# Hybrid attention block: scores of two pairs in one visit from pair 4 on, and the up tiles by token turned by DMA, with one transpose of the identity behind them

## The chip, the cores and the metric

The kernel runs on one core of one Trainium2 chip. The metric is the device time of one execution in microseconds (us), lower is better. Engines are named as in the profile: PE is TensorE (PEld its weight loads), DVE is VectorE, ACT is ScalarE, POOL is GpSimd, SP is SyncE, which here only issues transfers.

## The reference

Two layers (DEPTH = 2) over 256 tokens of 1024 values. Each layer projects x to three kinds of attention with 8 heads each, gates and merges their outputs, adds and normalises, and then runs a convolutional gated feed-forward block, adds and normalises again. Cut to what matters here:

```python
o_mla = _dense_causal_attention(q, k, kv[..., MLA_NOPE:], (MLA_NOPE + MLA_ROPE) ** -0.5, None)   # heads of 96
o_fox = _dense_causal_attention(f_q, f_k, f_v, HEAD_DIM ** -0.5, cumsum(log_f))                  # heads of 64
o_dsa = _dsa_attention(s_q, s_k, s_v, i_q, i_k, i_w, positions, slopes, topk)                    # heads of 64
# feed-forward: D_FF = 2816, CONV_WIDTH = 3
u = x @ w_up
gate, val = u[..., :D_FF], u[..., D_FF:]
conv = conv_b + sum(gp[:, j:j + seq] * conv_w[j] for j in range(3))   # gp: gate, padded by two tokens in front
y = (gelu(conv) * val) @ w_down
```

## The kernel before, in words

Every engine's program is written out by hand in one order, and engines meet through counting semaphores (`wait_ge`, `then_inc`). All large products are made in three matmuls, high by high, high by low and low by high part (`product`, L738 to L740), with the parts split by ACT (`split_hi`, L1248) and DVE (`split_lo`, L1607) for each weight panel of 128 x 2048 values. SP loads panels into a ring of 6 raw buffers; a slot is free when PE has used the panel six before.

**Attention.** The 24 heads form 12 pairs: pairs 0 to 3 are the fox heads (64 rows), 4 to 7 the MLA heads (96 rows), 8 to 11 the DSA heads (64 rows). PE runs through slots 0 to 27. In slots 0 to 23 it makes one gate tile (24 products), and behind it, where due, small plain fp32 work: `scores` of pair i in slot 2i + 1 (four matmuls in L1042, two passes each: for each of two token tiles one for each head of the pair), the probabilities' transposes for pairs 0 and 1 (L1057), and `values` of two pairs (L1080). Such a place, where PE leaves the products and comes back, is called a visit. Scores of every pair go to PSUM banks 0 and 1, so `scores(i)` waits until DVE has read pair i - 1. From pair 2 on the probabilities are turned by DMA: POOL splits the 32-bit words into two planes of 16 bits (`split_probs`, L2119), SP issues a transposing DMA (L698), and DVE or POOL joins the planes again. From slot 24 the branch panels follow.

**Feed-forward, up.** An up panel f gives 128 gate columns and 128 value columns. The first three panels are made by token (`up_by_token`: tokens in the rows of the result), because token tile 0 is normalised before tile 1. ACT copies their results to `u_tok` (L1372). PE then turns them into columns by 12 transposes (`turn_up`, L1146): 8 behind the last product by token, 4 behind panel 3. Panels 3 to 21 are made by column (`ffn_up`, 48 products each, moving x). For each panel ACT takes the first tap (`conv_first`, L1380), DVE the other two (`conv_rest`, L1868 and L1871), ACT the gelu (L1387), DVE multiplies (`hidden`, L1879), and both split the result (L1391, L1883). The same loops of ACT and DVE also split the weight panel two ahead, so a late step there delays weights.

## Time and profile before

| what | us |
|---|---|
| median of 3 runs (lowest to highest) | 825.98 (825.44 to 826.12) |
| the profiled execution | 826.03 |
| its span in the profile | 824.3 |
| PE busy | 812.5 (99%) |
| DVE busy | 596.5 (72%) |
| ACT busy | 469.6 (57%) |
| POOL busy | 177.3 (22%) |

The profile is of one execution. Its span is the time between the first and the last instruction; 1.73 us of the execution's 826.03 lie outside it. PE is busy nearly the whole span, and in the profile's chain of work that ended last it has 95%. A PE matmul row's duration is modelled and overlaps the next one's; what a product costs is the distance between the starts of two rows, called its pitch below.

### The profile page before, as it was taken

To read this page: it belongs to the slowest core of one execution; us is meant where nothing else is said; L and a number is where in the kernel's file an instruction comes from. 1 tells how busy PE (TensorE), PEld (TensorE's weight loads), DVE (VectorE), ACT (ScalarE), POOL (GpSimd) and SP (SyncE) were. 2 spreads that over 40 slices of the span, in tenths; PEclk is the share of its full clock that TensorE was granted. 3 is DMA by queue.
4 is the path that set the end of the run, shared out by engine and by line. 5 is a ranking of instruction groups with operands and counts; after the bars stand their busy time and mean duration, and the time that the engine had idled before them with its cause. 6 is when DMAs were issued, how large, how long until landed. Compare 5 with 4: busy or idle time off the path is not lost.

```text
span 824.3 us, 15624 instructions
## 1 busy us (share of the span) xinstructions
PE 812.5 (99%) x6215; PEld 759.0 (92%) x6215; DVE 596.5 (72%) x1012; ACT 469.6 (57%) x729; POOL 177.3 (22%) x193
## 2 busy tenths in 40 slices
PE   8999999999999999999999999999999999999996
PEld 7899999899899999988889999999998999999885
DVE  5675789878886777765676568998887587777555
ACT  5675876763446555543447578767544475555440
POOL 1502944439200000000000057333660000000000
PEclk9999999999999999999999999999999999999998
DMA  9959657767578776475846694778767776664731
GB/s 305 241 141 258 209 143 204 199 161 247 171 187 215 203 202 189 151 236 181 264 122 172 117 339 148 180 186 205 212 196 209 181 200 186 187 184 155 254 116 51
DMA packets 222266, 158.86 MB, mean 193 GB/s; under 512 B 64652, under 2 KB 196336, under 8 KB 221936
## 3 DMA queue, kind: packets, MB, share of 16 engines
q1 hardware_dynamic: 213120, 150.95, 65.2%
q10 hardware_dynamic: 9072, 6.90, 3.0%
q8 instruction: 49, 0.80, 0.4%
q14 instruction: 25, 0.20, 0.1%
HBM read 148.63 MB, written 1.06 MB: 182 GB/s over the span
## 4 chain that ended last, share of the span: by engine, by line
PE 95%; DVE 1%; SPq 1%; DMA 1%; ACT 1%; ACTq 1%; issue 0%; DVEq 0%
PE ps L738 29%; PE ps L740 29%; PE ps L739 29%; PE ps L1042 3%; PE ps L1080 2%; DMA raw<-w_in 1%; PE ps L817 1%; ACTq L1300 1%; DVE w_lo L1607 1%; ACT w_hi L1248 0%; PE ps L1004 0%; PE ps L1057 0%; PE ps L1146 0%; SPq L687 0%; DVE x_tok L1858 0%
## 5 line engine op out<-in xcount | busy, mean ns | idle before, releaser
L1607 DVE TENSOR_TENSOR w_lo<-raw,w_hi 128x2048 fp32r<-128x2048 f32 (+2 forms) x140 | 304.8, 2178 | 109.7 <-ACT w_hi L1248 109.5
L738 PE MATMUL ps<-xt_hi,w_hi 128*128 128x256 f32 x1232 | 346.0, 281 | 0.0
L739 PE MATMUL ps<-xt_lo,w_hi 128*128 128x256 f32 x1232 | 341.0, 277 | 0.0
L740 PE MATMUL ps<-xt_hi,w_lo 128*128 128x256 f32 x1232 | 341.0, 277 | 0.0
L1248 ACT ACTIVATE w_hi<-raw 128x2048 fp32r<-128x2048 f32 (+3 forms) x142 | 253.1, 1786 | 90.7 <-PE ps L740 67.9
L738 PEld LDWEIGHTS ps<-xt_hi,w_hi 128*128 128x128 f32 x1232 | 231.5, 188 | 5.8 <-issue 4.7
L739 PEld LDWEIGHTS ps<-xt_lo,w_hi 128*128 128x128 f32 x1232 | 231.5, 188 | 0.2
L740 PEld LDWEIGHTS ps<-xt_hi,w_lo 128*128 128x128 f32 x1232 | 231.5, 188 | 0.0
L738 PE MATMUL ps<-w_hi,ht_hi 128*128 128x512 f32 (+1 forms) x179 | 69.1, 386 | 0.0
L740 PE MATMUL ps<-w_hi,ht_lo 128*128 128x512 f32 (+1 forms) x179 | 69.0, 386 | 0.0
L739 PE MATMUL ps<-w_lo,ht_hi 128*128 128x512 f32 (+1 forms) x179 | 69.0, 386 | 0.0
L1380 ACT ACTIVATE cv<-ps,vec_t 128x256 f32<-128x256 f32 x44 | 20.8, 474 | 81.4 <-PE ps L740 77.8
L2148 POOL COPY km_t<-km_t 32x1792 f32<-32x1792 f32 x2 | 3.4, 1675 | 295.5 <-ACT km_t L1328 295.5
L1335 ACT ACTIVATE prob<-prob,least 128x128 f32<-128x128 f32 x96 | 42.5, 445 | 22.0 <-DVE least L1743 22.0
L738 PE MATMUL ps<-w_hi,xt_hi 128*128 128x256 f32 (+2 forms) x144 | 46.2, 321 | 0.6 <-DVE w_lo L1607 0.5
L740 PE MATMUL ps<-w_hi,xt_lo 128*128 128x256 f32 (+2 forms) x144 | 45.1, 313 | 0.0
L739 PE MATMUL ps<-w_lo,xt_hi 128*128 128x256 f32 (+2 forms) x144 | 45.0, 312 | 0.0
L1868 DVE SCALAR_TENSOR_TENSOR cv<-ps,vec_t,cv 128x255 f32<-128x255 f32 x44 | 21.3, 483 | 30.2 <-ACT cv L1380 29.9
L2179 POOL TENSOR_TENSOR merged<-merged,gated 128x256 f32<-128x256 f32 x32 | 40.2, 1287 | 5.3 <-DVE gated L1791 5.2
L740 PEld LDWEIGHTS ps<-w_hi,ht_lo 128*128 128x128 f32 x179 | 33.6, 188 | 6.7
L738 PEld LDWEIGHTS ps<-w_hi,ht_hi 128*128 128x128 f32 x179 | 33.6, 188 | 6.7
L739 PEld LDWEIGHTS ps<-w_lo,ht_hi 128*128 128x128 f32 x179 | 33.6, 188 | 6.7
(268 smaller groups left out, 1304.8 us busy)
## 6 DMA issues: line engine op xcount, KB each, us to landing
raw<-ffn_w_up SPq DMA_DIRECT2D x88, 512.0 KB, 5.2
raw<-w_in SPq DMA_DIRECT2D x84, 512.0 KB, 5.8
raw<-ffn_w_down SPq DMA_DIRECT2D x32, 512.0 KB, 4.2
raw<-w_branch SPq DMA_DIRECT2D x24, 512.0 KB, 4.6
raw<-w_out SPq DMA_DIRECT2D x16, 512.0 KB, 5.6
raw<-ffn_w_down SPq DMA_DIRECT2D x24, 256.0 KB, 3.0
decay<-decay_rows ACTq DMA_DIRECT2D x2, 1024.0 KB, 8.4
ln_g<-ln_g ACTq DMA_DIRECT2D x4, 512.0 KB, 3.6
```

Source lines behind the costliest of these rows:

```text
L738: pe.matmul(dst, a_hi, b_hi, start=first, stop=False)
L739: pe.matmul(dst, a_hi, b_lo, start=False, stop=False)
L740: return pe.matmul(dst, a_lo, b_hi, start=False, stop=last)
L817: ins = pe.transpose(ps[:, B_X[t][half], P * k:P * k + P], x_tok[:, t, P * kk:P * kk + P], ident[:])
L1042: ins = pe.matmul(ps[:, B_S[a], SPAN[t]], q[:, P * t:P * t + P], k[:, 0:P * (t + 1)], start=True, stop=True)
L1080: ins = pe.matmul(dst[HD * a:HD * a + HD, P * c:T], v, turned(i)[:, a, cols], start=c == 0, stop=c == 1)
L1248: ins = act.activation(panel_hi(l, p)[0:n, cols], panel_raw(l, p)[0:n, cols], ACT.Copy)
L1335: ins = act.activation(p, p, ACT.Exp, scale=-1.0, bias=least[:, i % 2, a, t:t + 1], accum_out=rsum[:, i % 2, a, t:t + 1])
L1380: act.activation(cv[:, buf, :], ps[:, B_UP[f % len(B_UP)], 0:T], ACT.Copy, scale=column(vec_t, V_CW + 2 * FT, f)).then_inc(s_conv_first_ta ...
L1607: ins = dve.tensor_tensor(low, panel_raw(l, p)[0:n, cols], panel_hi(l, p)[0:n, cols].bitcast(F32), ALU.subtract)
L1868: dve.scalar_tensor_tensor(cv[:, buf, 1:T], ps[:, B_UP[f % len(B_UP)], 0:T - 1], column(vec_t, V_CW + FT, f), cv[:, buf, 1:T], ALU.mult, A ...
L2179: pool.tensor_tensor(merged[:, u % KD, :], merged[:, u % KD, :], gated[:, u % NGATED, :], ALU.add).then_inc(s_merged_added, 1)
```

## The change

**Scores.** `PAIRED = range(4, 12)`: in the slot of an even pair i from 4 on, PE makes the scores of i and then of i + 1, in one visit. The odd pair writes to banks 2 and 3, which held the probabilities' transposes of pairs 0 and 1. DVE and ACT keep their slots.

**Up tiles.** `turn_up` is gone. POOL splits `u_tok` of each token tile into 16-bit planes (`split_up`), SP turns each tile by one transposing DMA (`cross_up`, behind the loads of panels 6 and 8), and POOL joins the planes into `u_feat` by 12 small copies (`join_up`). Behind the last product by token PE makes one transpose of the identity, whose result nobody reads, and goes on with panels 3 to 21. ACT and DVE take the tiles in the order 3, 4, 0, 5, 1, 6, 2, 7, ..., tiles 0 to 2 from SBUF.

```diff
+UP_ORDER = [3, 4, 0, 5, 1, 6, 2] + list(range(7, FT))
+UP_NO = [UP_ORDER.index(f) for f in range(FT)]
+PAIRED = range(4, PAIRS)
+B_S_ODD = (2, 3)
...
+        def score_bank(i, a):
+
+            return B_S_ODD[a] if i in PAIRED and i % 2 else B_S[a]
...
+            def cross_up(l, t):
+
+                sp.wait_ge(s_up_split, at("up_split", l, t + 1))
+                sp.dma_start_transpose(up_crossed[:, t], up_halves[:, t].rearrange("p u n -> p (u n)")).then_inc(s_up_crossed[t], 16)
...
+                    if p in (UP_AT + NLO, UP_AT + UP_BY_TOKEN - 1 + NLO):
+                        cross_up(l, p > UP_AT + NLO)
...
             def scores(l, i):
...
-                if i > 0:
+                if i > PAIRED.start + 1:
+                    pe.wait_ge(s_maxima_ready, at("maxima_ready", l, 2 * i - 2))
+                elif i == PAIRED.start + 1:
+                    pe.wait_ge(s_turned_even_ready, at("turned_even_ready", l, 2))
+                    pe.wait_ge(s_turned_odd_ready, at("turned_odd_ready", l, 2))
+                elif i > 0:
                     pe.wait_ge(s_maxima_ready, at("maxima_ready", l, 2 * i))
...
-                if f >= len(B_UP):
-                    pe.wait_ge(s_hidden_ready, at("hidden_ready", l, f - len(B_UP) + 1))
+                if f >= UP_BY_TOKEN + len(B_UP):
+                    pe.wait_ge(s_hidden_ready, at("hidden_ready", l, UP_NO[f - len(B_UP)] + 1))
+                elif f == UP_BY_TOKEN + len(B_UP) - 1:
+                    pe.wait_ge(s_up_tokens_ready, at("up_tokens_ready", l, NT * UP_BY_TOKEN))
...
                     for i in even_slot_pair(s, LAG_S):
-                        scores(l, i)
+                        if i not in PAIRED:
+                            scores(l, i)
+                        elif i % 2 == 0:
+                            scores(l, i)
+                            scores(l, i + 1)
...
-                turn_up(l, 0)
-                turn_up(l, 1)
-                ffn_up(l, 3)
-                turn_up(l, 2)
-                for f in range(4, FT):
+                pe.transpose(ps[:, B_R[0][1], 0:P], ident[:], ident[:])
+                for f in range(UP_BY_TOKEN, FT):
                     ffn_up(l, f)
...
-                for f in range(FT):
-                    if f >= 3:
+                for n, f in enumerate(UP_ORDER):
+                    if f >= UP_BY_TOKEN:
                         split_hi(*later(l, UP_AT + f, 2))
-                    if f >= 1:
-                        gelu(l, f - 1, (f - 1) % 2, f < 3)
-                    if f >= 2:
-                        hidden_hi(l, f - 2, f % 2)
-                    conv_first(l, f, f % 2)
+                    if n >= 1:
+                        gelu(l, n - 1, (n - 1) % 2, n < 3)
+                    if n >= 2:
+                        hidden_hi(l, n - 2, n % 2)
+                    conv_first(l, n, n % 2)
...
+            def split_up(l, t):
+
+                pool.wait_ge(s_up_tokens_ready, at("up_tokens_ready", l, UP_BY_TOKEN * (t + 1)))
+                pool.tensor_copy(up_halves[:, t], u_tok[:, t, :, :].rearrange("p f n -> p (f n)").bitcast(U16).rearrange(
+                    "p (n u) -> p u n", u=2)).then_inc(s_up_split, 1)
+
+            def join_up(l, f):
+
+                if f == 0:
+                    for t in range(NT):
+                        pool.wait_ge(s_up_crossed[t], 16 * (l + 1))
+                for t in range(NT):
+                    for i in range(2):
+                        src = up_crossed[:, t].rearrange("p (u b) k -> p u b k", u=2)[:, :, 2 * f + i, :]
+                        ins = pool.tensor_copy(u_feat[:, f, i, P * t:P * t + P].bitcast(U16).rearrange("p (k u) -> p u k", u=2), src)
+                ins.then_inc(s_up_joined, 1)
```

The order of PE's instructions in slots 17 to 19 of the first layer, before the change (sk_t and sq_t are the keys and queries of the DSA heads, L738 to L740 the products of the gate tiles):

```order
990 L1042 MATMUL ps<-sk_t,sq_t 128x128 x2
991 L1042 MATMUL ps<-sk_t,sq_t 128x256 x2
992 L738 MATMUL ps<-xt_hi,w_hi 128x256
...
1039 L740 MATMUL ps<-xt_hi,w_lo 128x256
1040 L1042 MATMUL ps<-sk_t,sq_t 128x128 x2
1041 L1042 MATMUL ps<-sk_t,sq_t 128x256 x2
1042 L738 MATMUL ps<-xt_hi,w_hi 128x256
```

The same place in the changed kernel, whose lines have other numbers (L1079 is the matmul of `scores`, L770 to L772 the products):

```order
989 L772 MATMUL ps<-xt_hi,w_lo 128x256
990 L1079 MATMUL ps<-sk_t,sq_t 128x128 x2
991 L1079 MATMUL ps<-sk_t,sq_t 128x256 x2
992 L1079 MATMUL ps<-sk_t,sq_t 128x128 x2
993 L1079 MATMUL ps<-sk_t,sq_t 128x256 x2
994 L770 MATMUL ps<-xt_hi,w_hi 128x256
```

The second pair's four matmuls moved ahead of 48 products and stand behind the first pair's with nothing between.

PE at the end of the products by token, first layer, before (the 8 transposes; 4 more follow 48 products later, in row 1737):

```order
1686 L739 MATMUL ps<-w_lo,xt_hi 128x256
1687 L740 MATMUL ps<-w_hi,xt_lo 128x256
1688 L1146 MATMUL ps<-ident,u_tok 128x128 x8
1689 L738 MATMUL ps<-xt_hi,w_hi 128x256
1690 L739 MATMUL ps<-xt_lo,w_hi 128x256
```

and in the changed kernel:

```order
1686 L771 MATMUL ps<-w_lo,xt_hi 128x256
1687 L772 MATMUL ps<-w_hi,xt_lo 128x256
1688 L1250 MATMUL ps<-ident 128x128
1689 L770 MATMUL ps<-xt_hi,w_hi 128x256
1690 L771 MATMUL ps<-xt_lo,w_hi 128x256
```

Twelve transposes became one, and the products by column follow it without another break.

ACT behind the last copy to `u_tok` in the changed kernel (L1279 is `split_hi`, L1412 `conv_first`, L1419 `gelu`, L1423 `hidden_hi`):

```order
209 L1403 ACTIVATE u_tok<-ps 128x256 x2
210 L1279 ACTIVATE w_hi<-raw 128x2048
211 L1412 ACTIVATE cv<-ps,vec_t 128x256
212 L1279 ACTIVATE w_hi<-raw 128x2048
213 L1419 ACT_TABLE_LOAD
214 L1419 ACTIVATE ge<-cv,vec_t 128x256
215 L1412 ACTIVATE cv<-ps,vec_t 128x256
216 L1419 ACTIVATE ge<-cv,vec_t 128x256
217 L1423 ACTIVATE ht_hi<-hf 128x256
218 L1412 ACTIVATE cv<-u_feat,vec_t 128x256
219 L1279 ACTIVATE w_hi<-raw 128x2048
```

Before, the first two tiles' steps stood between the `u_tok` copies and the first split; now a split comes first, and the tiles from `u_feat` stand between tiles of later panels, each ahead of a split.

## Rows read from the trace of the kernel before

**Rows 1.** The page: busy us, share and instructions of each engine.

```profile
PE 812.5 (99%) x6215; PEld 759.0 (92%) x6215; DVE 596.5 (72%) x1012; ACT 469.6 (57%) x729; POOL 177.3 (22%) x193
```

**Rows 2.** The view of waits: PE's longest behind its first instruction (total, times, longest).

```profile
PE ps L738 <- DVE w_lo L1607: 0.5, 1, 0.5
```

**Rows 3.** Timeline of PE, an MLA scores visit (start us, us, what).

```profile
139.87 0.28 PE L740 MATMUL ps<-xt_hi,w_lo 128*128 128x256 f32 x1
...
141.12 0.47 PE L738 MATMUL ps<-xt_hi,w_hi 128*128 128x256 f32 x1
141.42 0.28 PE L739 MATMUL ps<-xt_lo,w_hi 128*128 128x256 f32 x1
```

**Rows 4.** Timeline of PE, a DSA scores visit.

```profile
148.51 0.28 PE L740 MATMUL ps<-xt_hi,w_lo 128*128 128x256 f32 x1
148.71 0.93 PE L1042 MATMUL ps<-sk_t,sq_t 64*128 64x128 f32 x8
149.57 0.39 PE L738 MATMUL ps<-xt_hi,w_hi 128*128 128x256 f32 x1
149.79 0.28 PE L739 MATMUL ps<-xt_lo,w_hi 128*128 128x256 f32 x1
```

**Rows 5.** Timeline of PE, the up tiles' transposes and the products up to down.

```profile
248.38 0.28 PE L740 MATMUL ps<-w_hi,xt_lo 128*128 128x256 f32 x1
...
249.30 0.37 PE L738 MATMUL ps<-xt_hi,w_hi 128*128 128x256 f32 x1
...
254.73 0.28 PE L740 MATMUL ps<-xt_hi,w_lo 128*128 128x256 f32 x1
...
255.20 0.36 PE L738 MATMUL ps<-xt_hi,w_hi 128*128 128x256 f32 x1
...
353.23 0.39 PE L738 MATMUL ps<-w_hi,ht_hi 128*128 128x512 f32 x1
```

**Rows 6.** Timeline of PE, two transposes of key ropes between products.

```profile
60.89 0.28 PE L740 MATMUL ps<-xt_hi,w_lo 128*128 128x256 f32 x1
61.00 0.38 PE L1021 MATMUL ps<-ident,kr 128*32 128x128 f32 x2
61.14 0.37 PE L738 MATMUL ps<-xt_hi,w_hi 128*128 128x256 f32 x1
61.34 0.28 PE L739 MATMUL ps<-xt_lo,w_hi 128*128 128x256 f32 x1
```

**Rows 7.** Timeline of PE, one gate tile pair (48 products) between two visits.

```profile
95.66 0.88 PE L1057 MATMUL ps<-ident,prob 128*128 128x128 f32 x6
96.30 0.36 PE L738 MATMUL ps<-xt_hi,w_hi 128*128 128x256 f32 x1
...
102.12 0.93 PE L1042 MATMUL ps<-fk_t,fq_t 64*128 64x128 f32 x8
```

**Rows 8.** Windows: stretch and length, busy of PE, PEld, DVE, ACT, POOL, then PEclk, DMA, GB/s.

```profile
118.90:124.30 5.40, 5.40 (x48) 5.40 (x48) 5.16 (x17) 4.11 (x10) 1.89 (x3) 1.00 0.80 193
```

**Rows 9.** Timeline of ACT, the last copy to u_tok.

```profile
248.71 0.39 ACT L1372 ACTIVATE u_tok<-ps 128x256 f32<-128x256 f32 x1 [2.45 <-PE ps L740]
```

**Rows 10.** Groups of POOL instructions by form (count, busy us, mean ns, idle before).

```profile
L2119 POOL COPY prob_halves<-prob 128x768 uint16<-128x768 uint16 x24 | 19.3, 827 | 13.9 <-PE ps L1042 6.7 <-DVE prob L1754 6.3 <-ACT prob L1349 0.8
L2125 POOL COPY pts_odd<-halves_crossed 128x768 uint16<-128x768 uint16 x6 | 8.8, 1460 | 21.3 <-DMA halves_crossed<-prob_halves 21.3
```

**Rows 11.** Tile late_crossed: issue durations in ns (min/median/max), and landing in us.

```profile
L698 SPq DMA_TRANSPOSE late_crossed<-late_halves x16: 1212/1224/2103, 157.4 to 586.5; - x16
...
DMA to landing us min/median/max: 2.7/2.8/4.4
```

**Rows 12.** Timeline of DVE in the up loop: the second tap of two successive tiles.

```profile
260.67 0.48 DVE L1868 SCALAR_TENSOR_TENSOR cv<-ps,vec_t,cv 128x255 f32<-128x255 f32 x1
...
264.49 0.48 DVE L1868 SCALAR_TENSOR_TENSOR cv<-ps,vec_t,cv 128x255 f32<-128x255 f32 x1
```

**Rows 13.** Tile w_lo: duration of the DVE splits in ns (min/median/max).

```profile
L1607 DVE TENSOR_TENSOR w_lo<-raw,w_hi x140: 957/2289/2778, 16.7 to 802.4; 128x2048 fp32r<-128x2048 f32 x110, 128x1536 fp32r<-128x1536 f32 x24, 128x1024 fp32r<-128x1024 f32 x4, 128x768 fp32r<-128x768 f32 x2
```

More of the change, by code:

```diff
@@ L233, in build_program @@
         s_up_tokens_ready = sem("up_tokens_ready")
-        s_up_turned = sem("up_turned")
+        s_up_split = sem("up_split")
+        s_up_joined = sem("up_joined")
+        s_up_crossed = [sem(f"up_crossed_{t}") for t in range(NT)]
         s_conv_first_tap = sem("conv_first_tap")
@@ L413, in build_program @@
             sf("beside_hidden", [P, PADS[4]])
+            with ExitStack() as over:
+                so = sized(over)
+                so("under_up", [P, FT - 12, T])
+                u_feat = so("u_feat", [P, UP_BY_TOKEN, 2, T])
+                up_halves = so("up_halves", [P, NT, 2, UP_BY_TOKEN * 2 * P], U16)
             ht_hi = sf("ht_hi", [P, FT, T], F32R)
+            with ExitStack() as over:
+                so = sized(over)
+                so("under_crossed", [P, FT - 6, T])
+                up_crossed = so("up_crossed", [P, NT, 4 * UP_BY_TOKEN, P], U16)
             ht_lo = sf("ht_lo", [P, FT, T], F32R)
@@ L645, in halves @@
             if p < DOWN_AT:
-                return up_halves(l, s, p - UP_AT)
+                return up_columns(l, s, p - UP_AT)
             c, g = divmod(p - DOWN_AT, len(DOWN_K))
@@ L657, in first_panel, with up_psum, up_columns @@
             return pieces
-        def up_halves(l, s, f):
+        def up_psum(f, i):
+            if f < UP_BY_TOKEN:
+                return u_feat[:, f, i, :]
+            return ps[:, B_UP[f % len(B_UP)], T * i:T * i + T]
+        def up_columns(l, s, f):
             return [(view(s, KD, 2 * P)[:, :, P * i:P * i + P],
@@ L1041, in scores @@
                             q, k = spread_rows(sq_t, a)[:, j, :], spread_rows(sk_t, a)
-                        ins = pe.matmul(ps[:, B_S[a], SPAN[t]], q[:, P * t:P * t + P], k[:, 0:P * (t + 1)],
+                        ins = pe.matmul(ps[:, score_bank(i, a), SPAN[t]], q[:, P * t:P * t + P], k[:, 0:P * (t + 1)],
                                         start=True, stop=True)
@@ L1139, in up_by_token @@
                     turn_x(l, 1, 1, (1,))
-            def turn_up(l, f):
-                pe.wait_ge(s_up_tokens_ready, at("up_tokens_ready", l, UP_BY_TOKEN + f + 1))
-                for i in range(2):
-                    for t in range(NT):
-                        ins = pe.transpose(ps[:, B_UP[f % len(B_UP)], T * i + P * t:T * i + P * t + P],
-                                           u_tok[:, t, f, P * i:P * i + P], ident[:])
-                ins.then_inc(s_up_turned, 1)
             pe.wait_ge(s_const, N_CONST)
@@ L1201, in _ @@
                         else:
-                            pe.transpose(ps[:, B_PT[0], 0:P], ident[:], ident[:])
+                            pe.transpose(ps[:, B_S[0], 0:P], ident[:], ident[:])
                         values(l, g)
@@ L1737, in row_least @@
                     for t in range(NT):
-                        src, dst = ps[:, B_S[a], SPAN[t]], prob[:, i % 2, a, SPAN[t]]
+                        src, dst = ps[:, score_bank(i, a), SPAN[t]], prob[:, i % 2, a, SPAN[t]]
                         if b == FOX:
@@ L2041, in _ @@
                 split_lo(l, UP_AT + 4)
-                for f in range(FT):
-                    if f >= 3:
+                for n, f in enumerate(UP_ORDER):
+                    if f >= UP_BY_TOKEN:
                         split_lo(*later(l, UP_AT + f, 2))
-                    if f >= 1:
-                        hidden(l, f - 1, (f - 1) % 2, f < 3)
-                    if f >= 2:
-                        hidden_lo(l, f - 2, f % 2)
-                    conv_rest(l, f, f % 2)
+                    if n >= 1:
+                        hidden(l, n - 1, (n - 1) % 2, n < 3)
+                    if n >= 2:
+                        hidden_lo(l, n - 2, n % 2)
+                    conv_rest(l, n, n % 2)
                 for p in range(DOWN_AT, NP):
@@ L2180, in _ @@
                                        ALU.add).then_inc(s_merged_added, 1)
+                for t in range(NT):
+                    split_up(l, t)
+                for f in range(UP_BY_TOKEN):
+                    join_up(l, f)
     return nc
```

47 lines of the change are left out of this document (25 added, 22 removed).

## The prediction

> **What bounds the kernel now.** I read the page first: PE is busy 99% of the span [rows 1]. The view of waits says how little of the rest is waiting: once PE has begun, its longest wait is 0.5 us, once [rows 2]. So the kernel is a stream of PE instructions laid end to end. A change is worth what it takes out of that stream, unless it makes PE wait. I therefore read PE's timeline around each edited place, start to start.
>
> Between the starts of two products of 256 columns lies one of two pitches. In the up panels, from 255.20 to 353.23, stand 864 products by column; with 0.09 us for the slow first step that is 97.94 / 864 = 0.1134 us each [rows 5]. In the 48 products between 96.30 and 102.12, less about 0.09 us at either end, it is 5.64 / 48 = 0.1175 us [rows 7]. I use 0.113 and 0.118. The clock is not the difference: in a slow stretch behind an MLA visit it is granted in full (1.00, the 2.4 GHz level) [rows 8]. A stretch keeps its pitch from one interruption to the next. That is a second thing the change can touch, and the larger one.
>
> **Scores.** The change takes out four visits a layer: behind pairs 5, 7 (MLA) and 9, 11 (DSA).
>
> An MLA visit takes 139.87 to 141.12, less the last product's own 0.12, plus the first product's longer step, 0.30 less 0.12: 1.31 us [rows 3]. Its eight passes are four of 128 columns and four of 256, so one of each costs 1.31 / 4 = 0.33 us, and that is about their streaming time: nothing is lost at its ends. Merging saves 0.00 there. The stretches behind MLA visits are slow before and stay so.
>
> A DSA visit takes 148.51 to 149.57, less 0.11, plus 0.22 less 0.11 on the next step: 1.06 us [rows 4]. The passes are as long, but the two heads sit in different halves of the array and run together: four steps, two of each kind, are 2 x 0.33 = 0.66 us. So 0.40 us of each visit is its ends: 0.20 instead of 0.11 before it, the first weights, and 0.22 instead of 0.11 behind it. The second pair, directly behind the first, pays 0.66 and not its ends. Saved: 0.40 us. From below, the row excludes less than 0 (all its work was there before); from above, 0.40. I take 0.40, as the four steps' price comes from the same shapes. Two DSA visits a layer, two layers: 4 x 0.40 = 1.60 us.
>
> The waits of the merged visit ask for no more than before: pair i + 1 waits for the maxima of pair i - 1, on which PE waited in the same slot for pair i; banks 2 and 3 are free since pair 1. Earlier scores for the odd pair only let DVE start `row_least` sooner.
>
> **Up tiles, PE.** The 8 transposes: 248.38 to 249.30 less 0.12 is 0.80, the next step is 0.09 longer, and the three behind it together 0.01: 0.90 us. The 4: 254.73 to 255.20 less 0.11 is 0.36, plus 0.09 and 0.01: 0.46 us [rows 5]. Together 1.36 us a layer. In their place stands one transpose. The nearest row is two of them between products: 60.89 to 61.14 less 0.11, plus 0.20 less 0.11, is 0.23 us [rows 6]; one transpose is (0.80 - 0.36) / 4 = 0.11, so a visit of one costs about 0.13. Bounds: 0.02 (an identity that hides wholly) to 0.23. Saved 1.23 us a layer, 2.46 in all.
>
> **Up tiles, the long way round.** Its cover has to be checked, since it holds up ACT and DVE. Take the first layer, in which panel 3 would now start at about 248.6 and each panel takes 48 x 0.1134 = 5.44 us. The last `u_tok` copy ends at 249.1 [rows 9]. POOL is idle there; its split of 768 halves takes 0.83 [rows 10], so 1536 take 1.7: 250.8. SP has then issued panel 8, which waits for the products by token; a transpose of half this size takes SP 1.2 us to issue and lands in 2.8 (at most 4.4) [rows 11]. Twice that is at most 5.6 to 8.8: 256.4 to 259.6. Four joins of 256 halves, a third of 0.83 to 1.46 each [rows 10], give 257.5 to 261.5 for tile 0. ACT asks for it behind panel 4's tile, whose product ends near 259.6, so at about 262. Covered, by 0.5 to 4.5 us. The next raw load behind the second transpose on SP, of panel 9, waits for panel 3's product at 254.1 anyway; SP is free by 253.3. Tiles 1 and 2 follow 1.6 us apart and are asked for 7 us apart.
>
> Three extra tiles now stand between panels 4 and 7. A tile with a split takes ACT and DVE 3.82 us [rows 12]; one without, from its parts, about 2.3. The split that is late is that of panel 9: three tiles (1, 6, 2) stand between panel 5's tile (265.2) and it. They take 8.4 us, or 11.5 if each costs the full 3.82; ACT and DVE then need 4.6 us (0.4, 1.9 and 2.3) for the split: 278.2 to 281.3. PE wants it at 248.6 + 6 x 5.44 = 281.3. So the margin is 3.1 to 0.0 us. Panels 7 and 8 have 2 us or more. Cost taken: nothing.
>
> Beside POOL's copies a split by DVE has taken up to 2.78 instead of 2.29 us [rows 13]. The Trainium skill calls the port pair of VectorE and GpSimd an exclusive lock, against a DVE instruction with two SBUF inputs too (SBUF — State Buffer, SBUF: two separate sides). By it a split could lose one whole join, an estimate of 0.4 us, and with no margin left PE would wait as long in each layer: 0.8 us, and the sum would be 822.7. The row gives at most 0.49 us for a longer copy beside it, which the margin's upper part covers; I take no cost.
>
> **Sum.** 1.60 + 2.46 = 4.06 us. The profiled execution would go from 826.03 to 821.97; it stands 0.05 above the median, which would be **821.9 us** (-0.5%). This measurement tells about 0.2%, 1.65 us, from no change.
>
> **The rivals.**
>
> *The up panels in the slow pitch.* Behind the one transpose stand 19 x 48 = 912 products in a row, and the pitch that the first ones find lasts to the end of the stage. At 0.118 instead of 0.113 they cost 912 x 0.0045 = 4.1 us a layer: 826.0 with one layer, 830.1 with both. It decides as soon as both layers fall so: 8.2 lost against 4.06 won is slower than before. For it: behind six transposes that PE had waited for, the products stayed slow [rows 7], and the products by token just before are slow too. Against it: behind transposes that PE did not wait for, all six stretches by column are fast, two and eight and four of them [rows 5, 6], and the identity waits for nothing. One transpose alone between products by column stands nowhere. Chances: one layer 0.08, both 0.06. The Trainium skill gives one gap for a warm matmul, N / 2.4 plus 2.5 ns (TensorE: Matmul & The Clock Gate, Back-to-back issue gap), an estimate of 109 ns for 256 columns; by it there would be one pitch, and this rival would have no price and no chance. No stretch here is that fast, and there are two pitches; the rows decide.
>
> *A split comes late.* If the turned tiles come at 264 instead of 262, or DVE is slower, PE waits for panel 9, one for one beyond the margin: 0.5 us a layer, say. The wait may also throw the pitch: 13 panels, 624 products x 0.0045 = 2.8 us. 822.9 without that, up to 828.5 with it in both layers. For it: a margin that may be 0.0. Against: before, panel 5's split was about as close in the timeline, and PE did not wait. Chance 0.10, half of it with a thrown pitch.
>
> *The scores save nothing that lasts.* Either the merged visit costs its ends inside (PE drains between the pairs), or PE comes 0.8 us earlier to the branch panels, where it already stops for a moment in each layer, and waits that much longer for DVE and POOL. Then only the up tiles' gain stands: 825.98 - 2.46 = 823.5. Against: in the DSA slots DVE's timeline shows DVE waiting for PE's scores, so it would come earlier too, and POOL's work hangs on PE's values and DVE's probabilities. Chance 0.12.
>
> **How the numbers follow.** The forecast, with its terms' bounds (0.1 us on a transposed visit, 0.1 on a DSA visit, and short stretches that change pitch, 48 x 0.0045 = 0.2 us apiece), holds 821.2 to 822.8: chance 0.64. Scores without gain, 0.12, reach to 823.7. A late split without a thrown pitch, 0.05, reaches to 824.0. Low end 820.9 for visits that I priced too cautiously, high end 824.4: 0.81 inside. Outside: one slow layer (0.08) and the thrown pitch in one or both (0.05), 824.5 to 828.5, and both layers slow (0.06), 830. Faster by over 0.2% (below 824.3): 0.64 + 0.12 + 0.05 = 0.81. Within 0.2%: 0.08 + 0.03 = 0.11. Slower: 0.06 + 0.02 = 0.08.
>
> **What the changed profile would show.** DSA visits of 16 passes in one row, about 1.7 us from last product to first, eight score visits a layer. MLA visits of 16 rows, about 2.6 us. Behind the single transpose, 912 products that take 103.4 us from the first to the first product down (107.5 if slow, and then I am wrong). No PE wait at a panel of `ffn_w_up`; the DVE split of panel 9 ending before PE's start of it. Tile 0 joined before ACT asks. If instead the branch panels show PE waits of 0.5 us or more on DVE or POOL, the third rival is right.

## The result: slower, 830.81 us, and the profile after

| | before | after |
|---|---|---|
| median, us | 826.05 | 830.81 |
| lowest to highest | 825.44 to 826.99 (4 runs) | 828.28 to 831.87 (4 runs) |
| ratio, 95% interval | | 1.0054 (1.0043 to 1.0066) |
| the profiled execution | 826.03 | 828.28 |
| its span | 824.3 | 826.5 |

The forecast was 821.9. The change made the kernel 0.5% slower, and its four runs lie 3.6 us apart, those of before 1.6 (in the rounds of the experiments below the kernel before had times from 824.78 to 827.87). The profiled execution is the fastest of the four, so its trace shows the smaller part of the loss.

The page of the changed kernel, the line that answers to [rows 1]:

```profile
PE 814.8 (99%) x6193; PEld 762.3 (92%) x6193; DVE 599.0 (72%) x1012; ACT 468.6 (57%) x729; POOL 197.1 (24%) x221
```

PE has 22 instructions fewer and is busy 2.3 us longer. The longer time is no wait: the same kind of work got slower. The view of waits has little more than before [rows 2]:

```profile
PE ps L770 <- DVE w_lo L1639: 0.7, 2, 0.5
```

So I read PE's timeline at the places of [rows 5]. First layer of the changed kernel (start us, us, what): the single transpose, the first product by column, and the first product down.

```profile
248.30 0.28 PE L772 MATMUL ps<-w_hi,xt_lo 128*128 128x256 f32 x1
248.42 0.27 PE L1250 MATMUL ps<-ident 128*128 128x128 f32 x1
248.44 0.37 PE L770 MATMUL ps<-xt_hi,w_hi 128*128 128x256 f32 x1
...
281.07 0.28 PE L772 MATMUL ps<-xt_hi,w_lo 128*128 128x256 f32 x1
281.60 0.38 PE L770 MATMUL ps<-xt_hi,w_hi 128*128 128x256 f32 x1 [0.26 <-DVE w_lo L1639]
281.83 0.28 PE L771 MATMUL ps<-xt_lo,w_hi 128*128 128x256 f32 x1
...
352.45 0.39 PE L770 MATMUL ps<-w_hi,ht_hi 128*128 128x512 f32 x1
```

Second layer:

```profile
651.79 0.28 PE L772 MATMUL ps<-w_hi,xt_lo 128*128 128x256 f32 x1
651.91 0.27 PE L1250 MATMUL ps<-ident 128*128 128x128 f32 x1
651.93 0.36 PE L770 MATMUL ps<-xt_hi,w_hi 128*128 128x256 f32 x1
...
759.43 0.39 PE L770 MATMUL ps<-w_hi,ht_hi 128*128 128x512 f32 x1
```

The same 912 products take 352.45 - 248.44 = 104.01 us in layer 1 and 759.43 - 651.93 = 107.50 in layer 2. Less 0.09 us for the first step and divided by 912, the second is 0.1178 each from end to end: the slow pitch. The first is 0.1134 each, plus one stall at panel 9, where one step took 281.60 - 281.07 = 0.53 instead of 0.11, and the next 0.11 more than usual: 0.53 us lost together. The clock is granted in full in the slow stretch (window of layer 2; the column before the DMA share is the granted clock):

```profile
core 0: us, PE busy (x) PEld busy (x) DVE busy (x) ACT busy (x) POOL busy (x), PEclk, DMA share, GB/s
...
652.00:759.00 107.00, 107.00 (x911) 107.00 (x910) 76.97 (x102) 60.16 (x83) 8.84 (x13) 1.00 0.71 194
```

The merged DSA visit, answering to [rows 4]:

```profile
148.34 0.28 PE L772 MATMUL ps<-xt_hi,w_lo 128*128 128x256 f32 x1
148.54 1.58 PE L1079 MATMUL ps<-sk_t,sq_t 64*128 64x128 f32 x16
150.05 0.39 PE L770 MATMUL ps<-xt_hi,w_hi 128*128 128x256 f32 x1
150.28 0.28 PE L771 MATMUL ps<-xt_lo,w_hi 128*128 128x256 f32 x1
150.39 0.28 PE L772 MATMUL ps<-xt_hi,w_lo 128*128 128x256 f32 x1
150.51 0.28 PE L770 MATMUL ps<-xt_hi,w_hi 128*128 128x256 f32 x1
```

The visit costs 150.05 - 148.34, less 0.11, plus 0.23 less 0.11: 1.72 us, as forecast. But the 72 products behind it run at the slow pitch, 158.64 - 150.05 less 0.11 = 8.48 us or 0.1178 each, where behind a single DSA visit they ran fast. All four merged DSA visits of this trace are so, and all four in each of the other 16 traces below that keep the merged visits where they are here, 68 of 68. Behind the 16 single DSA visits of the traces of before and e2_up_alone the pitch was fast each time.

**Where 2.25 us come from.** From the last product by token to the first product down, layer 1 took 353.23 - 248.38 = 104.85 us before [rows 5] and takes 104.15 now: 0.70 gained. Layer 2 took 104.84 (652.22 to 757.06) and takes 107.64: 2.80 lost. The slots from the first MLA visit to the branch panels took 57.93 us in each layer before (117.42 to 175.35, 521.33 to 579.26) and now 57.71 and 57.70: 0.45 gained. That leaves +0.6 us elsewhere. Most of it is pitch again, at places that the change does not touch: the 96 products at the head of layer 2's features took 10.98 us before (436.01 to 446.99) and 11.39 now (435.18 to 446.57).

### The profile page after: what moved, and what is told of

The parts are those of the page before. It is cut to its first block, busy times and chain, and to the rows that moved or that the text cites. A ratio compares the mean times of both kernels' runs of the same rounds, so it can differ in the third digit from the quotient of the medians.

```text
span 826.5 us, 15612 instructions
## 1 busy us (share of the span) xinstructions
PE 814.8 (99%) x6193; PEld 762.3 (92%) x6193; DVE 599.0 (72%) x1012; ACT 468.6 (57%) x729; POOL 197.1 (24%) x221
## 3 DMA queue, kind: packets, MB, share of 16 engines
HBM read 148.63 MB, written 1.06 MB: 181 GB/s over the span
## 4 chain that ended last, share of the span: by engine, by line
PE 92%; DMA 2%; SPq 2%; DVE 1%; ACT 1%; issue 1%; DVEq 1%; POOL 0%; ACTq 0%; POOLq 0%
PE ps L770 29%; PE ps L771 28%; PE ps L772 28%; PE ps L1079 3%; PE ps L1117 2%; DMA up_crossed<-up_halves 1%; ACT w_hi L1279 1%; DMA raw<-w_in 1%; SPq L749 1%; PE ps L849 1%; DVE w_lo L1639 1%; SPq L717 0%; DVEq L1903 0%; PE ps L1036 0%; PE ps L1094 0%
## 5 line engine op out<-in xcount | busy, mean ns | idle before, releaser
L1639 DVE TENSOR_TENSOR w_lo<-raw,w_hi 128x2048 fp32r<-128x2048 f32 (+2 forms) x140 | 308.9, 2208 | 111.7 <-ACT w_hi L1279 111.4
L770 PE MATMUL ps<-xt_hi,w_hi 128*128 128x256 f32 x1232 | 347.0, 282 | 0.3 <-DVE w_lo L1639 0.3
L772 PE MATMUL ps<-xt_hi,w_lo 128*128 128x256 f32 x1232 | 343.0, 278 | 0.0
L1279 ACT ACTIVATE w_hi<-raw 128x2048 fp32r<-128x2048 f32 (+3 forms) x142 | 252.8, 1784 | 86.9 <-PE ps L772 69.7
L770 PEld LDWEIGHTS ps<-xt_hi,w_hi 128*128 128x128 f32 x1232 | 231.2, 188 | 5.5 <-issue 4.0
L772 PEld LDWEIGHTS ps<-xt_hi,w_lo 128*128 128x128 f32 x1232 | 233.4, 189 | 0.0
L770 PE MATMUL ps<-w_hi,ht_hi 128*128 128x512 f32 (+1 forms) x179 | 69.1, 386 | 0.0
L772 PE MATMUL ps<-w_hi,ht_lo 128*128 128x512 f32 (+1 forms) x179 | 69.0, 386 | 0.0
L1412 ACT ACTIVATE cv<-ps,vec_t 128x256 f32<-128x256 f32 x38 | 17.9, 470 | 71.6 <-PE ps L772 71.6
L770 PE MATMUL ps<-w_hi,xt_hi 128*128 128x256 f32 (+2 forms) x144 | 46.3, 321 | 0.7 <-DVE w_lo L1639 0.5
L772 PE MATMUL ps<-w_hi,xt_lo 128*128 128x256 f32 (+2 forms) x144 | 45.1, 313 | 0.0
L770 PEld LDWEIGHTS ps<-w_hi,ht_hi 128*128 128x128 f32 x179 | 33.6, 188 | 6.7
L772 PEld LDWEIGHTS ps<-w_hi,ht_lo 128*128 128x128 f32 x179 | 33.6, 188 | 6.6
L1901 DVE SCALAR_TENSOR_TENSOR cv<-ps,vec_t,cv 128x255 f32<-128x255 f32 x38 | 18.3, 481 | 25.6 <-ACT cv L1412 25.6
```

The lines of the kernel that those rows point to most:

```text
L770: pe.matmul(dst, a_hi, b_hi, start=first, stop=False)
L772: return pe.matmul(dst, a_lo, b_hi, start=False, stop=last)
L1279: ins = act.activation(panel_hi(l, p)[0:n, cols], panel_raw(l, p)[0:n, cols], ACT.Copy)
L1412: act.activation(cv[:, buf, :], up_psum(f, 0), ACT.Copy, scale=column(vec_t, V_CW + 2 * FT, f)).then_inc(s_conv_first_tap, 1)
L1639: ins = dve.tensor_tensor(low, panel_raw(l, p)[0:n, cols], panel_hi(l, p)[0:n, cols].bitcast(F32), ALU.subtract)
L1901: dve.scalar_tensor_tensor(cv[:, buf, 1:T], up_psum(f, 0)[:, 0:T - 1], column(vec_t, V_CW + FT, f), cv[:, buf, 1:T], ALU.mult, ALU.add)
```

## The experiments

Each kernel was timed in rounds beside the kernel before (5 to 12 runs each, the changed kernel 4) and profiled once. One slow layer costs 107.50 - 103.46 = 4.0 us, so a kernel's times fall into steps. The last two columns say what the one trace shows of the two layers' up stretches (its own time ahead), which is all that is seen directly; how many layers were slow in the other runs is inferred from their times. Under 826 us I count both layers as fast. Most kernels with slow layers have a gap of 2 us or more above such runs, f4_none has none, and some runs (830.37 of the change, for one) lie between the steps, which no trace explains. The rounds ran on four chips (e on the first, f and k on the second, g and h on the third, j on the fourth), so contrasts on one chip are the safer ones.

| label | between the by-token and by-column products | lowest, median, highest | ratio (95%) | traced run | layers 1, 2 |
|---|---|---|---|---|---|
| the change | 1 of the identity | 828.28, 830.81, 831.87 | 1.0054 (1.0043-1.0066) | 828.28 | fast, slow |
| e1_scores_alone | as before (8, then 4) | 825.3, 825.79, 826.7 | 0.9998 (0.9989-1.0007) | 825.79 | fast, fast |
| e2_up_alone | 1 of the identity | 824.06, 831.1, 833.03 | 1.0047 (1.003-1.0064) | 824.06 | fast, fast |
| e4_two | 2 of the identity | 823.63, 831.43, 832.17 | 1.0045 (1.0024-1.0065) | 832.06 | slow, slow |
| e3_eight | 8 of the identity | 827.75, 829.5, 829.91 | 1.0041 (1.0028-1.0054) | 827.75 | fast, slow |
| g1_banks | 8 of the identity, old banks | 829.51, 831.28, 833.01 | 1.0065 (1.005-1.008) | 833.01 | slow, slow |
| g3_waits | 8 of the identity, old waits | 824.25, 829.09, 833.22 | 1.0038 (1.0015-1.0061) | 833.22 | slow, slow |
| j2_copy | 8 of a copy of the identity | 824.97, 829.62, 833.21 | 1.0051 (1.0031-1.0071) | 824.97 | fast, fast |
| f2_half_rows | 2 matmuls of 64 rows | 824.27, 831.29, 833.02 | 1.0051 (1.0032-1.0071) | 828.15 | slow, fast |
| f4_none | nothing | 823.28, 826.35, 828.87 | 0.9997 (0.9984-1.0009) | 823.28 | fast, fast |
| f3_eight_four | 8, and 4 behind panel 3, of the identity | 825.48, 826.54, 826.84 | 1.0 (0.9991-1.0008) | 826.66 | fast, fast behind the 4 |
| j1_one_real | 1 of `u_tok` | 823.58, 824.54, 830.43 | 0.9989 (0.9975-1.0004) | 824.26 | fast, fast |
| k3_two_real | 2 of `u_tok` | 827.77, 830.57, 831.68 | 1.0056 (1.0044-1.0068) | 827.77 | slow, fast |
| k1_four_real | 4 of `u_tok` | 827.47, 831.05, 832.1 | 1.0053 (1.0036-1.007) | 832.1 | slow, slow |
| g2_data | 8 of `u_tok`, one bank | 824.55, 824.91, 828.21 | 0.9995 (0.9986-1.0004) | 824.83 | fast, fast |
| f1_real_eight | 8 of `u_tok`, old banks and waits | 824.57, 824.76, 828.1 | 0.9987 (0.9978-0.9995) | 824.94 | fast, fast |
| k2_one_spread | 1 of `u_tok`, tiles spread | 822.86, 825.41, 827.89 | 0.9996 (0.9983-1.001) | 827.88 | slow, fast |
| j3_spread | 4 of `u_tok`, tiles spread | 831.86, 832.23, 832.85 | 1.0073 (1.0061-1.0085) | 832.23 | slow, slow |

The theory, **pitch**: the loss is the 912 products behind the new transpose. The rivals: the scores, and the long way round of the tiles (late splits).

**The two halves of the change.** e1_scores_alone is the kernel before with the scores' hunks alone. e2_up_alone is the changed kernel with

```diff
-PAIRED = range(4, PAIRS)
+PAIRED = range(PAIRS, PAIRS)
```

> The kernel before with the paired scores visits alone; its up tiles are turned on PE as before. In the changed kernel's trace all four merged DSA visits are followed by 72 products at 0.118 instead of 0.113 us. Theory of the pitch: the visits give back 72 x 0.0045 = 0.32 us each, 1.3 us of the 1.6, and the time falls by about 0.3 us, to 825.5 to 825.9, which this measurement cannot tell from before. Rival, that the pairing as such makes PE wait in the branch panels: slower than before by 1 us or more. The prediction's own term (1.60 us saved) would give 824.4.

> The changed kernel with no pair merged: the change of the up tiles alone. Theory of the pitch: behind the single transpose one or both layers run their 912 products at the slow pitch, 4.1 us a layer, against 2.46 us saved: 827.5 with one, 831.5 with both, so clearly slower than before. Rival, that the scores carry the loss: 823.5. Rival, that a late weight split carries the loss: 824 to 825 with a stall of 0.4 us in each layer and no slow pitch.

The scores alone change nothing that can be measured. The up tiles alone carry the whole loss, and one kernel takes from 824.06 to 833.03 us, 9 us apart. In the 824.06 run both layers were fast; here layer 2's stretch begins with the same three instructions as the slow one above:

```profile
651.64 0.27 PE L1250 MATMUL ps<-ident 128*128 128x128 f32 x1
651.67 0.37 PE L770 MATMUL ps<-xt_hi,w_hi 128*128 128x256 f32 x1
651.88 0.28 PE L771 MATMUL ps<-xt_lo,w_hi 128*128 128x256 f32 x1
...
755.18 0.39 PE L770 MATMUL ps<-w_hi,ht_hi 128*128 128x512 f32 x1
```

103.51 us for 912 products. The same instructions at the same place run at either pitch: in the changed kernel's one trace the two layers differ, and the twelve times of e2_up_alone lie 9 us apart. Which pitch comes is open at each execution.

**More transposes of the identity.** The edit, with 8 or 2:

```diff
-                pe.transpose(ps[:, B_R[0][1], 0:P], ident[:], ident[:])
+                for _ in range(8):
+                    pe.transpose(ps[:, B_R[0][1], 0:P], ident[:], ident[:])
```

> The changed kernel with eight transposes of the identity in place of one. They cost PE 7 x 0.11 = 0.77 us more in each layer. Theory of the pitch: behind eight transposes that PE does not wait for the products are fast, as before the change; both layers gain 4.1 us where they were slow, so the kernel gets faster in spite of more work: 826.2 us, and the trace shows 912 products at 0.113 in both layers. With both fast a stall of 0.4 us at panel 9 should stand in both. Rival, that the long way round of the turned tiles costs the time: 1.5 us slower than the changed kernel, 832.3.

> The changed kernel with two transposes of the identity in place of one, 0.11 us more a layer. Theory of the pitch, if two are enough, as behind the two key-rope transposes: both layers fast, 824.8 us. If what throws the pitch is not the number of transposes but the long row of products by token ahead, two behave as one did: 828 to 832. Rival, that the route of the tiles costs the time: 831.

My form of the theory fell: transposes as such do not make the products fast. By their times, eight did not give both layers fast in any of 5 runs (the trace has the first one fast), two did in 2 of 12 (823.63 and 824.47).

**What stood there before.** Four variants of the same line:

```diff
-                pe.transpose(ps[:, B_R[0][1], 0:P], ident[:], ident[:])
# f1_real_eight
+                for f in range(2):
+                    pe.wait_ge(s_up_tokens_ready, at("up_tokens_ready", l, UP_BY_TOKEN + f + 1))
+                    for i in range(2):
+                        for t in range(NT):
+                            pe.transpose(ps[:, B_UP[f], T * i + P * t:T * i + P * t + P], u_tok[:, t, f, P * i:P * i + P], ident[:])
# f2_half_rows
+                for a in range(2):
+                    rows = slice(64 * a, 64 * a + 64)
+                    pe.matmul(ps[:, (B_R[0][1], B_UP[0])[a], 0:P], ident[rows, :], ident[rows, :], start=True, stop=True)
# f3_eight_four: 8 as in e3_eight, and 4 more ahead of ffn_up(l, 4)
# f4_none: the line is gone
```

> The changed kernel with, in place of the one transpose of the identity, the eight transposes of u_tok that stood there before the change, into their old banks; nobody reads them. Eight of the identity did not make both layers fast (one slow in the trace). Theory that their data, banks or waits set the pitch: both layers fast in every run, 825.5 to 826.5 us, spread under 1.5. Theory of chance, that transposes hand on or throw the pitch whatever they move: as with eight of the identity, 827 to 830, spread over 2 us, with a slow layer in most runs.

> The changed kernel with two plain matmuls of 64 rows, one in each half of the array, in place of the one transpose. In the trace all visits of 64 rows and all visits of values are followed by products at the fast pitch, with one exception, the merged visit. Theory that such a visit sets the pitch afresh: both layers fast in every run, some 0.3 us a layer dearer than the transpose: 824.2 to 825.2 us, faster than before. Theory of chance: a mixture from 824 to 832 as with one or two transposes.

> The changed kernel with eight transposes of the identity behind the products by token and four behind panel 3, the places and numbers of before the change. Theory that the second visit, between products by column, is what makes the rest fast: both layers fast in every run, 824.2 + 2 x 1.1 = 826.4 us, spread under 1.5. If both visits are left to chance: 828 to 832 with a wide spread. Rival, that the tiles' long way round costs time of its own: above 827 with all products fast and a stall in the trace.

> The changed kernel with nothing at all between the products by token and those by column. The by-token products end slow. Theory that a pitch is kept until something interrupts: both layers slow in every run, 831.8 us. Theory of chance: the turn from one kind of product to the other throws it too, a mixture from 823.9 to 832.

f1_real_eight, whose only difference from the change is what PE does in that gap, takes 6 us off it, though it gives PE seven transposes more in each layer. Its second layer:

```profile
651.72 0.28 PE L772 MATMUL ps<-w_hi,xt_lo 128*128 128x256 f32 x1
651.84 1.04 PE L1254 MATMUL ps<-ident,u_tok 128*128 128x128 f32 x8
652.63 0.37 PE L770 MATMUL ps<-xt_hi,w_hi 128*128 128x256 f32 x1
...
756.09 0.39 PE L770 MATMUL ps<-w_hi,ht_hi 128*128 128x512 f32 x1
```

103.46 us, fast, and no stall: the seven more transposes bring PE to panel 9 some 0.77 us later, when the split is there. The route by DMA is the same as in the change. It costs at most the stall of 0.53 us there and nothing here, so as the cause of the loss that rival is out. Visits of 64 rows are no cure either. With nothing between, runs spread over 5.6 us with no clear steps. Eight of the identity left the 48 products of panel 3 slow in both layers of f3_eight_four's trace, and four more, between products by column, made the rest fast: in the trace, and by their times (825.48 to 826.84) in all of its 11 runs.

**Banks, waits or data.** Eight each; the parts of f1_real_eight one at a time:

```diff
# g1_banks: the identity, to f1's banks and quarters, no waits
+                            pe.transpose(ps[:, B_UP[f], T * i + P * t:T * i + P * t + P], ident[:], ident[:])
# g2_data: u_tok, one bank, no waits
+                for n in range(8):
+                    pe.transpose(ps[:, B_R[0][1], 0:P], u_tok[:, 0, n // 4, P * (n % 2):P * (n % 2) + P], ident[:])
# g3_waits: the identity, one bank, f1's two waits
+                    pe.wait_ge(s_up_tokens_ready, at("up_tokens_ready", l, UP_BY_TOKEN + f + 1))
+                    for _ in range(4):
+                        pe.transpose(ps[:, B_R[0][1], 0:P], ident[:], ident[:])
```

> Eight transposes of the identity in place of one, now into the two banks (and their four quarters) that the eight of before the change wrote, without their waits. Before this, eight of the identity into one bank left layer 2 slow, and eight of u_tok with waits and two banks were fast in both layers, median 824.76. If the banks make the difference: as there, 824.8, spread under 1.5. If not: 829.5 as with the one bank.

> Eight transposes of u_tok (token tile 0 alone, for which PE has waited long before) into the one bank, without a wait. If what they read makes the difference: 824.8, spread under 1.5. If not: 829.5.

> Eight transposes of the identity into the one bank, with the two waits on ACT's copies in front of the first and the fifth, as the eight of before the change had them. If the waits make the difference, though PE hardly stands in them: 824.8, spread under 1.5. If not: 829.5.

With eight, what is transposed makes the difference: 10 of 11 runs lie within 824.6 to 825.4 with `u_tok`, none of 6 with the identity (g1_banks, the same chip) is under 829.5. Banks do nothing for it. The waits may do a little, 4 of 12 runs under 826.

**The buffer or the values; one, two, four.** j2_copy transposes `ident_2`, a copy of the identity in a buffer of its own; j1_one_real, k3_two_real and k1_four_real are g2_data with one, two and four.

> Eight transposes of a copy of the identity that lies in a buffer of its own: the same values, but the two operands are no longer one buffer. If it is the shared buffer that leaves the pitch to chance: median 824.9, spread under 1.5, as with u_tok. If it is the values (a matrix nearly all zeros): 829 to 831 with a wide spread, as with the identity itself.

> The changed kernel with its one transpose reading a tile of u_tok in place of the identity; all else equal. Eight transposes of u_tok (into either banks, with or without waits) were followed by fast products in nearly every run (medians 824.76, 824.91), eight of the identity were not. If what PE loads as weights there sets the pitch, one is enough: median 823.3 to 824.3 (0.77 us a layer less than with eight, and 0.4 us a layer given to the stall at panel 9), at most two runs of ten over 827. If it takes several: a mixture of 824, 828 and 832 like the changed kernel's.

> Two transposes of u_tok with the order of tiles of the changed kernel: the series one, two, four, eight. If all that counts is what is loaded, median 824.6. If the number counts too, a mixture or 832. Two of the identity gave 831.4.

> Four transposes of u_tok with the order of tiles of the changed kernel. With four and the spread order all five runs were slow in both layers (831.9 to 832.9). If the number of transposes did that: the same here, 832. If the order of ACT's and DVE's tiles did, though it cannot reach the first product: like one or eight of u_tok, median 824.5 to 825.

A copy gave both layers fast in 1 of 6 runs (its trace), no better than the identity itself, so a shared buffer is not it. And the number counts in a way that I cannot order: one of `u_tok` is fast in 9 of 12 runs, eight in 20 of 22, two and four in none of 12. With two, the data are no better than the identity was (2 of 12). Layer 1 of k1_four_real:

```profile
248.40 0.28 PE L772 MATMUL ps<-w_hi,xt_lo 128*128 128x256 f32 x1
248.52 0.60 PE L1251 MATMUL ps<-ident,u_tok 128*128 128x128 f32 x4
248.87 0.36 PE L770 MATMUL ps<-xt_hi,w_hi 128*128 128x256 f32 x1
...
356.37 0.40 PE L770 MATMUL ps<-w_hi,ht_hi 128*128 128x512 f32 x1
```

107.50 us, slow.

**The late split.** Both kernels have the turned tiles further apart:

```diff
-UP_ORDER = [3, 4, 0, 5, 1, 6, 2] + list(range(7, FT))
+UP_ORDER = [3, 4, 0, 5, 6, 1, 7, 8, 2] + list(range(9, FT))
```

> Four transposes of u_tok, and ACT and DVE take the tiles in the order 3, 4, 0, 5, 6, 1, 7, 8, 2, 9, so that two panels' tiles stand between two of the turned ones. The stall at panel 9 was 0.42 us in the changed kernel (the split ended 0.36 us after PE wanted it). Theory of the margin: no PE wait at any up panel, and with four transposes fast in nearly all runs 2 x 0.44 = 0.9 us less than with eight: 823.9 to 824.1. Rival, that a later panel is late instead: 824.5 with a stall at panel 10 to 13. If four are too few: a mixture up to 832.

> One transpose of u_tok and the tiles in the spread order. With one of u_tok the two layers' stalls at panel 9 were 0.16 and 0.17 us in the trace, each with a slow first step of 0.1 us behind it. Theory of the margin: no PE wait at an up panel in the trace where the layers are fast, and the median 0.5 us below that with one of u_tok (824.54), so 824.0. If the order spoils the pitch: 832 in every run.

j3_spread has four transposes of `u_tok` and was slow with this order and without it (k1_four_real), so it says nothing of the split. In k2_one_spread six of twelve runs, 822.86 to 824.26 (middle 823.7), have both layers fast; with the old order such runs (j1_one_real, another chip) have 823.58 to 824.56 (middle 824.5). Its traced run shows no wait at an up panel in the fast layer, whose 912 products take 103.46 us; in j1_one_real's trace each layer has a stall there and takes 103.74. By the traces the spread order is worth 0.28 us a layer, by the times some 0.8 in all; one slow layer costs 4.0.

**A way to a faster kernel that failed.** h1_joined is f1_real_eight and puts the values of groups 1 to 3 directly behind the merged scores:

```diff
-            return 4 * g + LAG_V + (4 if g < PAIRS // 2 - 1 else 3)
+            return 4 * g + LAG_V + (5 if g < PAIRS // 2 - 2 else 4 if g < PAIRS // 2 - 1 else 3)
...
-                        if s < SLOTS:
+                        if s % 2 and s < SLOTS:
+                            pass
+                        elif s < SLOTS:
```

> The version with eight transposes of u_tok, and in it the values of groups 1 to 3 moved 24 products later, directly behind the merged scores visits of slots 13, 17 and 21, without the transpose of the identity ahead of them. By the trace this takes out, three times a layer, the transpose (0.20 us), the ends of a visit (about 0.2), and 72 products at the slow pitch (0.32), since visits of values are always followed by fast products: 6 x 0.7 = 4.2 us less than 824.8, so 820.6, 0.6% faster than before. Rival, that the values come 2.8 us too late for DVE and POOL and PE waits for them at the branch panels: 822 to 825. Rival, that in such a long visit the exit is slow: 822.5.

833.51 us (831.07 to 834.18), ratio 1.0086 (1.0074 to 1.0098). The pitch did mostly what was hoped (fast behind five of the six joined visits of the trace), but the values came 24 products later and ACT and DVE with them. Its longest entry in the view of waits:

```profile
PE ps L770 <- DVE w_lo L1645: 6.8, 5, 2.5
```

PE's timeline at the longest of them (start us, us, what, and the idle time before):

```profile
156.53 0.28 PE L772 MATMUL ps<-xt_hi,w_lo 128*128 128x256 f32 x1
159.32 0.36 PE L770 MATMUL ps<-xt_hi,w_hi 128*128 128x256 f32 x1 [2.51 <-DVE w_lo L1645]
159.51 0.28 PE L771 MATMUL ps<-xt_lo,w_hi 128*128 128x256 f32 x1
159.63 0.32 PE L772 MATMUL ps<-xt_hi,w_lo 128*128 128x256 f32 x1
159.75 0.41 PE L770 MATMUL ps<-xt_hi,w_hi 128*128 128x256 f32 x1
159.97 0.41 PE L771 MATMUL ps<-xt_lo,w_hi 128*128 128x256 f32 x1
```

Two windows behind it (columns as above):

```profile
159.50:163.00 3.50, 3.50 (x19) 3.50 (x19) 3.40 (x14) 3.50 (x9) 2.22 (x3) 0.53 0.57 213
163.00:166.50 3.50, 3.50 (x31) 3.42 (x30) 2.09 (x1) 3.06 (x6) 0.00 (x0) 0.98 0.65 126
```

Behind a wait of 2.5 us the products stand 0.21 us apart and the granted clock of the window is 0.53, the 1.2 GHz level. Some twenty steps of 0.21 instead of 0.11 us cost 2 us more on top of the wait. In layer 2 the same wait stood there (2.77 us from start to start) with the clock at 1.00 behind it, but the products, fast ahead of the wait, were slow (0.118) behind it. PE stood before a weight split that DVE started late.

## Why the prediction was wrong, step by step

**MLA visits, 0.00 saved: right.** The merged visit takes 2.61 us, twice the 1.31 of [rows 3], and the products behind are slow as before.

**DSA visits, 0.40 saved each: the visit right, what lies behind it not.** It was priced at 1.06 + 0.66 = 1.72 and measured 1.72. But each gave back 72 x 0.0045 = 0.32 us of pitch, so 0.08 is left of 0.40. The slots gained 0.22 us a layer where 0.80 was forecast. The text allowed for "short stretches that change pitch" at 0.2 us apiece, once or twice, not for every one in the same direction. The third rival had the right size, 823.5, by a wrong mechanism: neither drain nor branch panels.

**The transposes, 1.23 saved a layer: right.** Layer 1's stretch is 0.70 us shorter with a stall of 0.53 in it: 1.23.

**The long way round: tile 0 hidden, as forecast.** POOL's timeline in the changed kernel, its second split and the twelve joins:

```profile
249.06 1.47 POOL L2158 COPY up_halves<-u_tok 128x1536 uint16<-128x1536 uint16 x1 [6.80 <-ACT u_tok L1403]
260.52 7.47 POOL L2169 COPY u_feat<-up_crossed 128x256 uint16<-128x256 uint16 x12 [9.99 <-DMA up_crossed<-up_halves]
```

ACT's, the first tap of tile 0:

```profile
262.19 0.51 ACT L1412 ACTIVATE cv<-u_feat,vec_t 128x256 f32<-128x256 f32 x1 [0.17 <-POOL u_feat L2169]
```

SP's queue, the second transposing DMA:

```profile
252.28 4.39 SPq L717 DMA_TRANSPOSE up_crossed<-up_halves  x1
```

The second transposing DMA could start only at 252.28, behind SP's last load, took 4.39 us to issue where I had 2.4, and landed at 260.4, past my 256.4 to 259.6. ACT waited 0.17 us for the tile, and PE did not notice.

**The margin at panel 9, 3.1 to 0.0: it was -0.4.** ACT took panel 5's tile at 265.12 and tile 2 at 276.92. The three steps between took 11.8 us, over my upper bound of 11.5, while POOL's joins and DVE's work slowed each other, as DVE's timeline shows (the last row is the split of panel 9):

```profile
264.55 2.54 DVE L1639 TENSOR_TENSOR w_lo<-raw,w_hi 128x2048 fp32r<-128x2048 f32 x1 [0.66 <-ACT w_hi L1279]
267.01 0.63 DVE L1912 TENSOR_TENSOR hf<-ge,u_feat 128x256 f32<-128x256 f32 x1
267.57 0.63 DVE L1917 TENSOR_TENSOR ht_lo<-hf,ht_hi 128x256 fp32r<-128x256 f32 x1
...
279.26 2.29 DVE L1639 TENSOR_TENSOR w_lo<-raw,w_hi 128x2048 fp32r<-128x2048 f32 x1 [0.77 <-ACT w_hi L1279]
```

The split took 2.54 us instead of 2.29 and the two products 0.63 instead of 0.42, together 0.67 us, without which the three steps would have stayed inside the bound; one of POOL's copies beside it took 2.51 us (the median is 0.49). The split of panel 9 ended at 281.55, and PE had wanted it at 281.18. So the second rival came true at its price without a thrown pitch, 0.53 us, in a layer that stayed fast. The Trainium skill's port lock (SBUF — State Buffer, SBUF: two separate sides) fits these rows, with 0.67 where I had taken an estimate of 0.4 from it and then left it out. Layer 2 has no stall: at the slow pitch PE asks for panel 9 later.

**The pitch of the up panels: the step that failed.** I wrote that it was against the slow pitch that "behind transposes that PE did not wait for, all six stretches by column are fast", and gave it 0.14. The rows behind that were of two, four and eight transposes, all of real data, and four of the six came out of a fast stretch. I had also read the six transposes of [rows 7] as a place where the products "stayed slow". They were fast ahead of that visit (0.1133 each up to 94.60) and slow behind it, and in layer 2 of the same trace the same visit left them fast:

```profile
500.39 0.37 PE L738 MATMUL ps<-xt_hi,w_hi 128*128 128x256 f32 x1
...
506.02 0.93 PE L1042 MATMUL ps<-fk_t,fq_t 64*128 64x128 f32 x8
```

By the sum of [rows 7] that is (5.63 - 0.18) / 48 = 0.1135 each, against 0.1175 in layer 1. So the trace of before already held one place with both pitches, and the chance of a slow layer behind a new visit could not be read off six cases that all came out fast. The runs show that the identity in the same number is not fast, that one stretch can come either way in the same kernel, and that it decided the result: one slow layer in the profiled run, 828.28, and by their times two or nearly two in the others. The price was right: 4.1 us a layer and 830.1 with both, measured 4.0 and a median of 830.81. The gap that the rival takes from the Trainium skill (TensorE: Matmul & The Clock Gate, Back-to-back issue gap) is given there for an isolated matmul. The estimate of 109 ns made from it is met by no long stretch of 256-column products here: the shortest pitch is 113. With both layers fast almost the same PE work gives 823.63 (e4_two's best run). So 821.9 would have been missed there too, by 1.15 us for the DSA visits (0.45 gained, not 1.60) and 0.5 for the stall, but inside the range. Even then the number would have held by a draw of the pitch, not by the reasoning that it could not come slow.

## What to carry to other kernels

When PE is busy 99%, its instructions' own pitch is a cost like any other: before a visit is removed or moved, look at how fast the long run behind it goes, and count that run's length times the difference (912 x 0.0045 us) against the visit (0.9 us). A behaviour seen in six stretches that differ from the new one in number and data has not been seen for the new one; give it a chance that reflects this, look whether the same place differs between the layers of one trace, and time such a kernel many times, since one profile shows one draw. Of the versions run here f1_real_eight (the change with the eight old transposes, unread) is the only one whose interval lies below the kernel before, 0.9987 (0.9978 to 0.9995); j1_one_real has the lower median, 824.54, with three of twelve runs 2.4 to 5.9 us above it.

## What the runs showed of the hardware that was not expected

- The pitch of 256-column products at the full granted clock is 0.1134 or 0.1178 us. In each of the 34 traced stretches of 912 products with nothing between, all 19 panels have the pitch of the first. Which one it is varies between executions, and the odds depend on what PE did just before: by their times (under 826 us), both layers were fast in 20 of 22 runs behind eight transposes of data, in 9 of 12 behind one with the old order and 6 of 12 with the spread one, in 5 of 12 with nothing between, in 8 of 57 behind one, two or eight of the identity or its copy, and in none of 17 behind two or four of data.
- A merged DSA visit of 16 passes of 64 rows left the next 72 products slow (0.1178 us) in 68 of 68 cases, one of 8 passes left the products fast (0.1134) in 16 of 16.
- In the changed kernel, a DVE split and a POOL copy beside one another took 2.54 us instead of 2.29 and 2.51 instead of 0.49.
- What stays open: why identity and data differ, and why one and eight transposes of data differ from two and four. The stretch ahead does not tell: the by-token products end slow in 37 of the 40 traced layers, and the three that end fast (layer 2 of e3_eight and of k2_one_spread, layer 1 of g1_banks) were followed by slow, fast and slow products. Their last gap (0.116 to 0.122 us ahead of fast stretches behind transposes or nothing, 0.117 to 0.120 ahead of slow ones, f2_half_rows aside) overlaps. The first step of the stretch is a sign, not a cause: behind transposes, 0.206 or 0.207 us stood only ahead of fast products, 0.200 to 0.203 ahead of both. Nothing here says by what mechanism a pitch is set or kept.
